# The full exponential of the attention scores goes to a buffer in SBUF, with rings of three for its high and low parts

## The reference, cut to what matters

```python
s = jnp.einsum("bqkgd,bskd->bkgqs", qblk, kf) * scale
p = jax.nn.softmax(s, axis=-1)
return jnp.einsum("bkgqs,bskd->bqkgd", p, vf)
```

## Time and profile before

| what | us |
|---|---|
| median of 3 runs (2590.25 to 2593.92) | 2591.84 |
| the profiled execution | 2592.71 |
| its span | 2590.9 |
| TensorE busy | 2477.0 (96%) |
| VectorE busy | 1692.4 (65%) |
| ScalarE busy | 1194.2 (46%) |
| GpSimd busy | 1101.8 (43%) |

### The profile page before, as it was taken

One profiled execution on the slowest core, in us unless ns is written; L12 is line 12 of the kernel. 1 busy time (PEld: TensorE's weight loads), 2 busy tenths in 40 slices (PEclk: granted clock), 3 DMA queues, 4 the chain that ended last, 5 costly groups with the idle time before them and its releaser, 6 DMA issues. The chain is left out here.

```text
span 2590.9 us, 40706 instructions
## 1 busy us (share of the span) xinstructions
PE 2477.0 (96%) x14413; PEld 2243.1 (87%) x14413; DVE 1692.4 (65%) x2527; ACT 1194.2 (46%) x2187; POOL 1101.8 (43%) x936
## 2 busy tenths in 40 slices
PE   5999999999999899999999989999899999999998
PEld 2899999999999887778878867799899999988886
DVE  5047456556558458787787767626977777776775
ACT  5223323323324246766666667645544444443442
POOL 1123132222223353433343233733667777756554
PEclk9999999999999999999999999999999999999999
DMA  9611111111111110010020010242122222245654
GB/s 328 207 35 45 36 52 44 37 43 44 37 43 30 50 34 9 11 54 9 9 65 9 1 55 27 91 119 74 48 72 76 76 76 76 76 159 204 222 199 142
DMA packets 193130, 195.66 MB, mean 76 GB/s; under 512 B 23516, under 2 KB 155772, under 8 KB 193020
## 3 DMA queue, kind: packets, MB, share of 16 engines
q1 hardware_dynamic: 191804, 189.52, 23.0%
q10 hardware_dynamic: 1216, 4.72, 0.5%
HBM read 162.22 MB, written 31.99 MB: 75 GB/s over the span
## 5 line engine op out<-in xcount | busy, mean ns | idle before, releaser
L395 PE MATMUL proj_ps<-act_hi,w_hi 128*128 128x384 f32 x1152 | 406.6, 353 | 3.3 <-ACTq L748 3.3
L397 PE MATMUL proj_ps<-act_hi,w_lo 128*128 128x384 f32 x1152 | 387.1, 336 | 0.0
L396 PE MATMUL proj_ps<-act_lo,w_hi 128*128 128x384 f32 x1152 | 386.9, 336 | 0.0
L571 POOL CAST w_hi<-w_raw 128x1024 fp32r<-128x1024 f32 x48 | 79.2, 1650 | 563.9 <-PE proj_ps L397 523.9
L1960 DVE TENSOR_TENSOR probs_lo<-mix_ps,probs_hi 128x512 fp32r<-128x512 f32 x324 | 222.9, 689 | 138.8 <-ACT mix_ps L1758 135.1
L2921 DVE SCALAR_TENSOR_TENSOR conv<-up,conv_t,conv 128x127 f32<-128x127 f32 (+4 forms) x264 | 242.1, 945 | 59.1 <-ACT conv L2701 53.5
L1757 ACT ACTIVATE probs_hi<-mix_ps 128x512 fp32r<-128x512 f32 x324 | 193.5, 597 | 174.8 <-PE mix_ps L1546 173.5
L395 PEld LDWEIGHTS proj_ps<-act_hi,w_hi 128*128 128x128 f32 x1152 | 217.6, 189 | 11.3 <-issue 4.3
L396 PEld LDWEIGHTS proj_ps<-act_lo,w_hi 128*128 128x128 f32 x1152 | 217.5, 189 | 2.8
L397 PEld LDWEIGHTS proj_ps<-act_hi,w_lo 128*128 128x128 f32 x1152 | 217.0, 188 | 0.0
L2969 DVE TENSOR_TENSOR sums_hi<-gated_raw,sums_hi 128x384 fp32r<-128x384 f32 x66 | 145.1, 2201 | 81.8 <-ACT sums_hi L2778 81.7
(11 more groups left out here) (341 smaller groups left out, 6895.7 us busy)
## 6 DMA issues: line engine op xcount, KB each, us to landing
w_raw<-in_w_down SPq DMA_DIRECT2D x66, 512.0 KB, 3.3
w_raw<-in_w_in SPq DMA_DIRECT2D x64, 512.0 KB, 3.8
w_raw<-in_w_up SPq DMA_DIRECT2D x44, 512.0 KB, 4.3
ada_w<-in_ada_w SPq DMA_DIRECT2D x7, 2048.0 KB, 15.8
gated_raw<-gated_scratch SPq DMA_DIRECT2D x66, 192.0 KB, 3.5
q_k_dec<-in_ada_w SPq DMA_DIRECT2D x5, 2048.0 KB, 7.9
gated_scratch<-gated SPq DMA_DIRECT2D x22, 288.5 KB, 2.1
gated_scratch<-gated SPq DMA_DIRECT2D x22, 287.5 KB, 2.1
```

The source lines that it names most:

```text
L395: nc.tensor.matmul(out, w_hi, x_hi, start=(k == 0), stop=False)
L396: nc.tensor.matmul(out, w_hi, x_lo, start=False, stop=False)
L397: return nc.tensor.matmul(out, w_lo, x_hi, start=False, stop=last)
```

## The change

The second exponential is written to a new SBUF buffer PF of two slots, x % 2, and the low part is taken from there. PH and PL have three slots in place of four. So a bank of scores is free for chunk x + 3 after the second exponential of x (`ex_done`), not after its low part (`lo_done`); the exponentials and low part of x wait for `weighted` of x - 3 (before: x - 4); and the second exponential of x waits for the low part of x - 2.

```diff
-        PH = sb("probs_hi", [P, 4, 512], F32R)
-        PL = sb("probs_lo", [P, 4, 512], F32R)
+        PH = sb("probs_hi", [P, 3, 512], F32R)
+        PL = sb("probs_lo", [P, 3, 512], F32R)
+        PF = sb("probs", [P, 2, 512])
...
                     if x >= 3:
-                        pe.wait_ge(lo_done, x - 2)
+                        pe.wait_ge(ex_done, x - 2)
...
-                    nc.tensor.matmul(bank, V1[:, c, :], PH[:, x % 4, :], start=(i == 0), stop=False)
-                    nc.tensor.matmul(bank[0:HEAD, :], V2[:, c, :], PH[:, x % 4, :], start=False, stop=False)
-                    nc.tensor.matmul(bank, V1[:, c, :], PL[:, x % 4, :], start=False, stop=last).then_inc(pv_done, 1)
+                    nc.tensor.matmul(bank, V1[:, c, :], PH[:, x % 3, :], start=(i == 0), stop=False)
+                    nc.tensor.matmul(bank[0:HEAD, :], V2[:, c, :], PH[:, x % 3, :], start=False, stop=False)
+                    nc.tensor.matmul(bank, V1[:, c, :], PL[:, x % 3, :], start=False, stop=last).then_inc(pv_done, 1)
...
                     act.wait_ge(st_done, x + 1)
-                    if x >= 4:
-                        act.wait_ge(pv_done, x - 3)
+                    if x >= 3:
+                        act.wait_ge(pv_done, x - 2)
                     bank = ps[:, B_ST + x % 3, :]
-                    nc.scalar.activation(PH[:, x % 4, :], bank, ACT.Exp, scale=SCALE)
-                    nc.scalar.activation(bank, bank, ACT.Exp, scale=SCALE).then_inc(ex_done, 1)
+                    nc.scalar.activation(PH[:, x % 3, :], bank, ACT.Exp, scale=SCALE)
+                    if x >= 2:
+                        act.wait_ge(lo_done, x - 1)
+                    nc.scalar.activation(PF[:, x % 2, :], bank, ACT.Exp, scale=SCALE).then_inc(ex_done, 1)
...
                     dve.wait_ge(ex_done, x + 1)
-                    if x >= 4:
-                        dve.wait_ge(pv_done, x - 3)
-                    nc.vector.tensor_tensor(PL[:, x % 4, :], ps[:, B_ST + x % 3, :], PH[:, x % 4, :].bitcast(F32), ALU.subtract).then_inc(lo_done, 1)
+                    if x >= 3:
+                        dve.wait_ge(pv_done, x - 2)
+                    nc.vector.tensor_tensor(PL[:, x % 3, :], PF[:, x % 2, :], PH[:, x % 3, :].bitcast(F32), ALU.subtract).then_inc(lo_done, 1)
```

## The result

The changed kernel takes 2639.45 us (median of 4 runs, 2633.88 to 2641.71) beside 2592.06 us of the kernel before on the same chip: a ratio of 1.0176, 95% interval [1.0161, 1.019]. It is slower by 47 us; 24 were forecast, and 2639.45 lies just inside the upper end of the range, 2640.

What follows compares the result with a forecast made beforehand. The prediction took TensorE to bound the attention stage, so only its waits count. Tail 15, key steps 6, most steps 1 and clock 2 made +24 us on the profiled 2592.7, less 0.9: 2616 us, range 2600 to 2640.

Steps and rivals of the forecast that it cites:

- The bank's release: Score banks freed earlier for TensorE: 0, since TensorE has already waited for a younger low part.
- the destination: ScalarE's second exponential writing SBUF in place of a bank: 0, at most 11 us, hidden by ScalarE's idle time.
- the rings: PH and PL with three slots: 0, since the order of TensorE's matmuls covers the tighter waits.
- the tail: 1603.8 to 1666.6 us: GpSimd and 38 low parts exclude each other, 79.2 us needed, +15 (bounds +4.5, +39).
- most steps: 950 to 1085 us and their like: collisions with short GpSimd instructions, covered by VectorE's idle time; +1, 0 to +5.
- the key steps: Three steps making the next heads' keys: low parts and GpSimd work exclude each other, low keys later; +6, 0 to +9.
- the clock: Attention stage: one or two more stretches partly at 1.2 GHz after longer TensorE waits; +2, 0 to +6.
- B: Rival: slack takes most up; only three late low parts, half the key steps and 1 us lost; 2600 us, chance 0.2.
- D: Rival: these collisions don't come, or only where nobody waits; 2592 us, chance 0.06.
- E: Rival: faster, as earlier bank release lets TensorE run ahead of VectorE; 2578, likelier 2585 us, chance 0.04.
- A: The forecast itself: GpSimd and low parts exclude each other, the tail pays in full; 2616 us, chance 0.6.
- C: Rival: the queues feed on each other; tail 30, key steps 9, rest and clock 9; 2640 us, chance 0.1.

Runs made afterwards that it cites:

- 4: The changed kernel, but TensorE again waits for the low part of x-3 before writing a bank: 2635.96 us, ratio 1.0164.
- 3: The changed kernel, but VectorE takes a maximum of the bank and PH instead of the low part, and TensorE waits for it: 2593.28 us, ratio 0.9992.
- 1: The kernel before, with PH and PL cut to three slots and the waits for weighted sums one chunk tighter: 2594.18 us, ratio 1.0011.
- 2: The kernel before with three-slot PH and PL, and the second exponential, still in the bank, waiting for the low part of x-2: 2594.3 us, ratio 1.0006.
- 5: The changed kernel, with VectorE's row maxima of the last head's steps all put ahead of the low part: 2632.72 us, ratio 1.0148.
- 7: The changed kernel, with GpSimd's weight splits and mix splits each issued as four quarter-length instructions: 2625.23 us, ratio 1.0136.
- 7's control: The kernel before, with GpSimd's weight splits and mix splits in the same quarters: 2600.08 us, ratio 1.0038.

## Why the prediction was right in its mechanism and half in its size

**Right: what costs nothing.** The bank's release (4), the destination (3: 599 ns a piece), the rings (1) and ScalarE's wait (2) were each put at 0, and each is 0 as far as can be told: to within about 5 us for the last three, some 10 for the release. The Trainium skill (ScalarE: Activation LUTs, Step-by-step: what each stage is for) says that ScalarE is quicker into PSUM; the runs don't agree: 596 and 598 ns into a bank, 598 and 599 into SBUF, over 324 each.

**Right: the mechanism.** The low part kept its clean time and got a maximum of 3.16 us, as the row of L2969 had it. A case of step 4, changed kernel, start and length in us:

```profile
1009.57 2.72 POOL L1274 TENSOR_TENSOR w_lo<-w_raw,w_hi 128x1024 fp32r<-128x1024 f32 x1
...
1009.95 2.89 DVE L1963 TENSOR_TENSOR probs_lo<-probs,probs_hi 128x512 fp32r<-128x512 f32 x1
...
1015.03 0.50 PE L1533 MATMUL mix_ps<-keys_hi,q_t_hilo 128*128 128x512 f32 x1 [1.96 <-DVE row_max L1950]
```

The low part ends 0.55 us after the split, having begun 0.38 us behind it: it queues, it does not share. This is what the Trainium skill's rule of the lock (SBUF — State Buffer, SBUF: two separate sides) says, and the trace agrees for the subtraction, which with one input in a bank has 695 ns at most in experiments 2 and 3, beside the same GpSimd work. What neither the prediction nor "held for the whole instruction" has is that a low part that begins in the last 0.2 us of a GpSimd instruction takes no more than 0.75 us (49 of the 324): not every meeting costs.

**Mis-sized: the tail, "+15".** It measured +23.8 by the stretch (86.6 us for 62.8; forecast 79.2), and +24.9 by steps 31 to 35. The failed step is the sum of exclusive work, 56.4 + 38 x 0.60, taken as the length, and both of its halves were wrong. GpSimd's busy time grew by 9.2 us (from 56.4 to 65.6), not by 22.8: a low part costs GpSimd 0.24 us in the mean, not 0.60. And the sum holds only if GpSimd always has something to do. It has not: its idle time grew from 6.4 to 21.0 us, by 14.6. Timeline of a case in the tail, changed kernel:

```profile
1630.45 1.55 POOL L1352 CAST act_hi<-rope_ws 128x1152 fp32r<-128x1152 f32 x1
1632.08 2.64 POOL L1354 TENSOR_TENSOR act_lo<-rope_ws,act_hi 128x1152 fp32r<-128x1152 f32 x1
1632.12 3.15 DVE L1963 TENSOR_TENSOR probs_lo<-probs,probs_hi 128x512 fp32r<-128x512 f32 x1
...
1635.30 0.69 DVE L1967 TENSOR_TENSOR inv_sum_check<-mix_ps,inv_sum 64x512 f32<-64x512 f32 x1
...
1636.03 0.69 DVE L1950 TENSOR_REDUCE row_max<-mix_ps 128x1 f32<-128x512 f32 x1
...
1636.77 0.50 PE L1533 MATMUL mix_ps<-keys_hi,q_t_hilo 128*128 128x512 f32 x1 [3.23 <-DVE row_max L1950]
...
1639.17 0.63 PE L1533 MATMUL mix_ps<-keys_hi,q_t_hilo 128*128 128x512 f32 x1
...
1645.61 0.40 POOL L1322 CAST q_stage_max<-qkv 128x256 fp32r<-128x256 f32 x1 [7.03 <-PE mix_ps L1509]
```

One low part is held 3.15 us; behind it in VectorE's queue stand the check of the inverse (0.69) and the row maximum (0.69); TensorE stands 3.23 us for that maximum. TensorE is then late with this step's transposes of the queries with their maxima (L1509), and GpSimd, whose second staging (L1322) writes the tile that those transposes read, idles 7.03 us and only then goes on (such waits of L1322 make 19.6 us in the tail, 9.2 before). A hold costs TensorE time, and TensorE's lateness gives GpSimd idle time, which then is missing for its queue. The sum of exclusive work knows neither. The prediction named the row maxima as "late next" but gave them no term; with them in front (5) the tail is 78.3 us, and 79.2 were forecast. That agreement is luck: there GpSimd is busy 68.1 us, 11.7 more than before, and the rest of the 15.5 us is idle time. Nor is the sum a bound: in quarters (7) the forecast's own sum would be 63.5 us of GpSimd's work and 40 x 0.60 = 87.5, and 81.6 were measured. A part of the low parts' time, then, excludes nobody; which part stays open.

**Mis-sized: "about 0" for most steps, taken as +1.** It measured about +12. The failed step is the mean: 36% of low parts meeting an instruction of 0.5 us on average. Holds are not average. Step 4 alone lost 3.2 us behind one 2.7 us split at its start, and steps 14, 16, 19, 20, 23 and 28 another 6.3; the other steps lose 0.1 us each. The mean over 135 us hid that the few long instructions lie at a step's end or start, just ahead of the row maxima that TensorE asks for next. In steps 14 and 23 the held instruction is not even a low part but a norm product, which has two SBUF inputs in both kernels. Step 14, before and after:

```profile
1215.34 1.78 DVE L1906 TENSOR_TENSOR qkv<-qkv,qk_rstd 128x320 f32<-128x320 f32 x1
...
1224.87 2.69 DVE L1909 TENSOR_TENSOR qkv<-qkv,qk_rstd 128x320 f32<-128x320 f32 x1
```

GpSimd's split begins 0.6 us ahead of step 14 before and 0.1 after, so more of it is left when the norm product comes, and TensorE's wait for the row maximum behind it grows from 0.5 to 1.4 us. That it is the single hold is shown by 7, where most of this loss goes with more work rather than less.

**Nearly right: the key steps, "+6".** +3.6 in the profiled run, but the three steps vary between runs: step 26 took 27.3 us before and 26.1 after, yet 30.6 in the runs of 4 and 5; steps 8 and 17 lost 3.3 and 3.7 there. By those it would be 10.3. They vary without the collisions too: in the kernels whose low part reads a bank step 26 takes 24.5 to 27.3 us and step 17 24.6 to 27.5. So this share isn't known to better than some 3 us a step. Step 26 may explain most of the distance from the profiled run, 2633.9, to the median, 2639.5; what tips it isn't known. It has no split in front of it, for which the prediction gave it nothing.

**Too small: the clock, "+2".** The number of stretches at 1.2 GHz (matmul of 0.63 us, as at 1639.17 above) in the stage went from 4 of 13.7 us together to 9 of 30.7 us. The stretch behind the 3.23 us wait, changed kernel (columns as in the earlier trace rows):

```profile
1636.00:1641.00 5.00, 4.23 (x12) 3.13 (x12) 4.38 (x7) 1.09 (x2) 2.50 (x3) 0.66 0.28 105
```

A granted clock of 0.66 is a part at 1.2 GHz, the rest at 2.4; each such stretch came right behind a wait of TensorE. 17 us more at half speed, if TensorE was the bound in all of them, are up to 8.5 us; they lie inside the step lengths above. Two facts keep this from being more than a bound: experiment 1, within 5 us of before, has 10.2 us of it, and 7's control, 8 us slower, 23.9. It was never changed by itself. "One or two more" was wrong by a factor of about three, as were the waits that it rested on (row maxima 26.3 us for 11.4).

**The rivals.** B (slack takes most up, 2600) fell with the tail at 86.6, which should be under 70 for it. D and E fell with the maximum of 3.16 and with L1546's unchanged 0.7 us. What came was the mechanism of A with most of the size of C: "the queues feed on each other", tail 30 (measured 25), key steps 9 (4 to 10), the rest and the clock 9 (12). The measured median lies 0.6 us inside the end of the range that was drawn for it, and two of the four runs lie outside: that the range holds is luck. C had the right reason in its one sentence, row maxima behind held subtractions, and got 0.1 where A got 0.6. It deserved more: the earlier trace rows show that row maxima, not low parts, were already what TensorE waited for most (11.4 us against 2.2), so any delay on VectorE's queue had to arrive there without cover.

## What to carry to other kernels

Before a VectorE operation gets its second SBUF input, look at what GpSimd does beside it: the input in a bank was what kept 324 subtractions at 0.69 us, and it cost nothing there. Price a collision by the longest GpSimd instruction that can stand in front of it and by what is queued behind the held instruction, above all where TensorE already waits for that queue; neither the mean wait nor the sum of exclusive work sees it. An expected gain from freeing a buffer sooner is first looked for as a wait at the instruction that takes the buffer; here it was 0.7 us before and after.

## What the runs showed of the hardware that was not expected

- The two engines' turns aren't fully exclusive: in quarters, GpSimd's 63.5 us (as in the control) and 40 low parts of 0.60 us fit into 81.6 us, where the sum is 87.5; in the changed kernel's tail 38 low parts add 9.2 us to GpSimd's busy time, 0.24 each.
- Whether a low part is held depends on where it begins. In the changed kernel 126 of 324 begin inside a GpSimd instruction. The 75 held ones all have more than 0.2 us of it left, and end 0.54 to 0.56 us after its end, however long it is (up to 2.6 us left; 3.16 us for the longest low part). The other 51 take at most 0.75 us: 49 have 0.2 us or less left, and two begin within 1 ns of the GpSimd instruction's start.
- A cut GpSimd instruction pays for each piece: four of 128x256 take 3.3 us for some 2.4 us of one of 128x1024, about 0.3 us for each of the three further instructions, in the control; in the changed kernel a piece took 912 ns in the mean, for 773.
